# An expert layer on one core: U is split two tiles ahead, ScalarE draws eight one-hot rows per tile, gates are stored in parts

## What is computed

```python
def peer_layer(xn, w_pq, sub_keys, expert_u, expert_v):
    qp = (xt @ w_pq).reshape(t, 8, 2, 128)               # 8 heads, two half queries
    scores = einsum('thpd,hpkd->thpk', qp, sub_keys)      # 128 keys per half
    s_top, i_top = top_k(scores, 16)                      # 16 of each half
    cand = s_top[:, :, 0, :, None] + s_top[:, :, 1, None, :]
    cand_idx = i_top[:, :, 0, :, None] * 128 + i_top[:, :, 1, None, :]
    best, pos = top_k(cand, 16)                           # 16 experts per head
    idx = take_along_axis(cand_idx, pos)
    gate = softmax(best)
    h = gelu(einsum('lkd,ld->lk', expert_u[idx], xb))     # 128 experts per token
    return einsum('lk,lkd->ld', gate * h, expert_v[idx])  # of 16384 experts
```

## Time and profile before

| | before |
|---|---|
| median of 3 runs | 3444.5 us (3442.72 to 3448.07) |
| profiled execution | 3439.6 us, span 3437.8 us |
| TensorE busy | 2902.1 us (84%), 15338 matmuls |
| VectorE busy | 1979.8 us (58%) |
| ScalarE busy | 1083.6 us (32%) |
| GpSimd busy | 824.4 us (24%) |
| mean granted TensorE clock | 0.915 of full speed |
| HBM traffic | 488.49 MB read, 88.21 MB written, 168 GB/s |

### The profile page before, as it was taken

The page is one execution under the profiler, slowest core; times in us unless marked ns, Lnnn a source line. Parts: engine busy times, 40 slices in busy tenths (PEclk is TensorE's granted clock), DMA queues, the critical chain, the costliest instruction groups (busy, mean ns, idle before and its releaser), DMA issues. The chain is left out here.

```text
span 3437.8 us, 40584 instructions
## 1 busy us (share of the span) xinstructions
PE 2902.1 (84%) x15338; PEld 2541.8 (74%) x15338; DVE 1979.8 (58%) x3415; ACT 1083.6 (32%) x1745; POOL 824.4 (24%) x643
## 2 busy tenths in 40 slices
PE   5787669969997878888799999799894869599987
PEld 4787438769996878887688888587673659488877
DVE  4324443337996777645677777545995642444432
ACT  3323442223323323322233333366222432222221
POOL 0002110003325776544423232034330010000000
PEclk8898879989998999999899999899995779799999
DMA  2102012233436776787999999467234532322222
GB/s 105 74 0 76 2 49 98 76 131 126 141 101 197 270 272 237 290 295 274 334 352 357 353 352 354 143 179 230 98 116 139 152 104 85 110 92 93 96 96 82
DMA packets 224065, 578.72 MB, mean 168 GB/s; under 512 B 34896, under 2 KB 126928, under 8 KB 194096
## 3 DMA queue, kind: packets, MB, share of 16 engines
q1 hardware_dynamic: 185184, 434.44, 37.2%
q0 software_dynamic: 36864, 134.23, 10.5%
q10 hardware_dynamic: 1872, 8.13, 0.7%
HBM read 488.49 MB, written 88.21 MB: 168 GB/s over the span
## 5 line engine op out<-in xcount | busy, mean ns | idle before, releaser
L40 PE MATMUL pe_ps<-hh,pe_uh 128*128 128x384 f32 x1024 | 353.5, 345 | 30.9 <-DVE pe_ul L1318 14.4
L41 PE MATMUL pe_ps<-hl,pe_uh 128*128 128x384 f32 x1024 | 347.0, 339 | 0.0
L42 PE MATMUL pe_ps<-hh,pe_ul 128*128 128x384 f32 x1024 | 346.5, 338 | 0.0
L40 PE MATMUL pe_ps<-pe_vh,pe_whi 128*128 128x512 f32 x768 | 300.8, 392 | 22.2 <-DVE pe_vl L1471 22.2
L41 PE MATMUL pe_ps<-pe_vl,pe_whi 128*128 128x512 f32 x768 | 300.4, 391 | 0.0
L42 PE MATMUL pe_ps<-pe_vh,pe_wlo 128*128 128x512 f32 x768 | 300.3, 391 | 0.0
L1279 POOL DMA_INDIRECT pe_gu<-in_u_rows,pe_urow x128 | 186.5, 1457 | 216.1 <-DVE pe_gu L1432 195.2
L1287 POOL DMA_INDIRECT pe_gv<-in_v_w,pe_vrow x128 | 151.7, 1185 | 353.6 <-DVE pe_acc L1441 339.9
L1432 DVE SCALAR_TENSOR_TENSOR pe_gu<-pe_gu,pe_xs 128x1024 f32<-128x1024 f32 x128 | 155.3, 1223 | 122.2 <-DMA pe_gu<-in_u_rows,pe_urow 122.2
L40 PEld LDWEIGHTS pe_ps<-hh,pe_uh 128*128 128x128 f32 x1024 | 196.4, 192 | 34.3 <-ACT pe_uh L1164 19.6
L40 PE MATMUL sc_ps<-hh,sc_wh 128*128 128x512 f32 x512 | 200.0, 391 | 12.6 <-DVE sc_wl L2515 12.6
(11 more groups left out here) (459 smaller groups left out, 7416.3 us busy)
## 6 DMA issues: line engine op xcount, KB each, us to landing
xu<-in_u_w SPq DMA_DIRECT2D x64, 1024.0 KB
pe_v_raw<-in_v_w SPq DMA_DIRECT2D x64, 1024.0 KB, 8.5
sc_raw<-in_sc_w SPq DMA_DIRECT2D x32, 1024.0 KB, 4.9
hidden_scratch<-pe_hs SPq DMA_DIRECT2D x64, 384.0 KB
gate_scratch<-pe_stage SPq DMA_DIRECT2D x6, 4096.0 KB, 19.7
pe_hw<-hidden_scratch SPq DMA_DIRECT2D x64, 384.0 KB
pe_gate<-gate_scratch SPq DMA_DIRECT2D x64, 384.0 KB
gf_raw<-in_gdn_w SPq DMA_DIRECT2D x24, 1024.0 KB, 6.8
```

The lines of the kernel that those rows point to most:

```text
L40: pe.matmul(out, lh, rh, start=start, stop=False)
L41: pe.matmul(out, lh, rl, start=False, stop=False)
L42: return pe.matmul(out, ll, rh, start=False, stop=stop)
```

## The change

- **Split ahead** (`AHEAD` = 2): ScalarE splits tile t+2 before the Gelus of tile t, VectorE makes its low half where it made that of t+3, and SP loads tile t+4 at tile t instead of t+5.
- **Stages**: `A_END` is 22 for 20 and `B_END` 46 for 44, so 22, 24 and 18 tiles. The transposes of the sparse tokens and their copy `xs` move ahead (tile 17 on TensorE, tile 18 on ScalarE).
- **One-hot rows**: ScalarE makes two `second` rows of each group (`DRAWN` = 2, eight a tile) for the next tile: Square(j - iota), then Relu(1 - that). VectorE makes the other eight. GpSimd makes none; it only fetches.
- **Gates in parts**: the 4,096 KB of 64 tokens go in four transfers, over the next three tiles, each ahead of that tile's hidden store.
- **Slots**: from the 85th U row on, five slots instead of three. The rows left after stage B are spread evenly over the 18 tiles.
- **V**: tiles 0 and 1 are loaded at U tiles 57 and 58 and weighed and split at 60 to 63, 2 and 3 are loaded at U tiles 62 and 63, the residual x after all V tiles. The fetched V rows are spread over tiles 2 to 63; before, four came ahead of tile 2.

```diff
@@ constants @@
-    A_END, B_END = 20, 20 + TD // PER
-    POOLED = (1, 2, 1, 2)
+    A_END, B_END = 22, 22 + TD // PER                 # AHEAD, DRAWN = 2, 2
+    EARLY, PARTS = (B_END - A_END) * EACH, 4
+    MORE = EARLY + 4 * EACH
+    def u_slot(s):
+        return s % GU if s < MORE else (s - MORE) % (GU + 2)
@@ SP @@
+                def keep_g(n, part):
+                    if part == 0:
+                        sp.wait_ge(staged, (n + 1) * (GT // Q))
+                    rows = slice(part * NKEYS // PARTS, (part + 1) * NKEYS // PARTS)
+                    sp.dma_start(g_dram[n][:, rows, :], stage[n % 2][:, rows, :]).then_inc(g_out[n % 2], 16)
+                def keep_some(r):
+                    n = r // 4 - 1
+                    for part in ((0, 1), (2,), (3,), ())[r % 4] if n >= 0 else ():
+                        keep_g(n, part)
-                        load_u(t + 5, r + 5, 0)
-                        keep_h(t, r)
-                        if r % 4 == 3:
-                            sp.wait_ge(staged, j * (BODY * Q) + (r + 1) * Q)
-                            sp.dma_start(g_dram[j * 2 + r // 4], stage[r // 4][:]).then_inc(g_out[r // 4], 16)
+                        load_u(t + 2 + AHEAD, t + 2 + AHEAD, 0)
+                        keep_some(t - A_END)
+                        keep_h(t, t)
...
+                    if t in (NU - 7, NU - 6):
+                        load_v(t - NU + 7, t - NU + 7, 0)
                     keep_h(t, t)
+                    if t >= NU - 2:
+                        sp.wait_ge(wv_lo, t - NU + 3)
+                        sp.wait_ge(v_lo, t - NU + 3)
+                        load_v(t - NU + 4, t - NU + 2, 0)
@@ ScalarE @@
+                def draw(it, e):
+                    if it == B_END - A_END:
+                        return
+                    if e:
+                        act.wait_ge(drawn[1], it + 1)
+                    elif it:
+                        act.wait_ge(drawn[3], it)
+                    for b in range(2):
+                        for m in range(DRAWN):
+                            tok = it * PER + (2 * e + b) * Q + m
+                            last = act.activation(gap[:, b, m, :], iota[:], ACT.Square, scale=-1.0, bias=jT[:, tok:tok + 1])
+                    last.then_inc(gap_ok, 1)
+                    act.wait_ge(gap_ok, 2 * it + e + 1)
+                    for b in range(2):
+                        act.activation(second[2 * e + b][:, 0:DRAWN, :], gap[:, b, :, :], ACT.Relu, scale=-1.0,
+                                       bias=iota[:, 1:2]).then_inc(drawn[2 * e + b], 1)
                     for r in range(BODY):
+                        split_u(t + AHEAD, t + AHEAD, 16 * ((t + AHEAD) // 2 + 1))
                         for e in range(UB):
                             gelu(t, t, e, 16 * (t // 2))
-                            if e == UB - 1:
-                                split_u(t + 3, t + 3, 16 * ((t + 3) // 2 + 1))
...
+                            draw(it + 1, e)
@@ GpSimd: the loop with L1297 to L1307 goes @@
+                    if u_last(s):                      # dot of the slot's last row
+                        pool.wait_ge(dot_ok, u_last(s))
+                    elif s >= GU:                      # first use of slots 3 and 4
+                        pool.wait_ge(g_out[1], 16 * PARTS * (TD // GT // 2))
...
+                for s in range(NS):
                     fetch_u(s)
@@ VectorE @@
-                                if m >= POOLED[q]:
+                                if m >= DRAWN:
...
-                        low_u(t + 3, t + 3)
+                        low_u(t + AHEAD, t + AHEAD)
...
-                    for s in range(EACH):
-                        dot((t - A_END) * EACH + s)
+                    if t in (NU - 4, NU - 3):
+                        weigh(t - NU + 4, t - NU + 4, 16)
+                    if t in (NU - 2, NU - 1):
+                        low_v(t - NU + 2, t - NU + 2)
+                    for s in range(upto(NS - EARLY, NU - B_END, t - B_END), upto(NS - EARLY, NU - B_END, t - B_END + 1)):
+                        dot(EARLY + s)
@@ TensorE @@
-                                pe.wait_ge(pooled[q], j * BODY + r + 1)
+                                pe.wait_ge(drawn[q], j * BODY + r + 1)
```

More of the change, by code:

```diff
@@ L993, in peer, with u_turn, u_last, upto @@
     ND, TD = PEER_DENSE, PEER_DENSE * P
-    NS, GU, GV, EACH = PEER_H * PEER_K, 3, 8, 3
+    NS, GU, GV, EACH, AHEAD, DRAWN = PEER_H * PEER_K, 3, 8, 3, 2, 2
     rest = slice(TD, T)
     NU = NKEYS // UB
-    A_END, B_END = 20, 20 + TD // PER
+    A_END, B_END = 22, 22 + TD // PER
     BODY = 8
-    POOLED = (1, 2, 1, 2)
+    EARLY, PARTS = (B_END - A_END) * EACH, 4
+    MORE = EARLY + 4 * EACH
+    def u_slot(s):
+        return s % GU if s < MORE else (s - MORE) % (GU + 2)
+    def u_turn(s):
+        return sum(u_slot(b) == u_slot(s) for b in range(s))
+    def u_last(s):
+        return max((b + 1 for b in range(s) if u_slot(b) == u_slot(s)), default=0)
+    def upto(s, steps, i):
+        return -(-s * i // steps)
     with Phase(nc, "pe") as ph:
@@ L1012, in peer @@
         urow, vrow = (ph.sb(n, [P, NS], U32) for n in ("urow", "vrow"))
-        dots, gs, wts = (ph.sb(n, [P, NS]) for n in ("dots", "gs", "wts"))
+        dots, gs = (ph.sb(n, [P, NS]) for n in ("dots", "gs"))
+        gap = ph.sb("gap", [P, 2, DRAWN, NKEYS])
         area = Arena(nc, ph, 80 * 1024 + 768, "arena")
@@ L1056, in peer @@
         wlo = [area.sb(f"wlo{i}", [P, UB, TD], F32R) for i in range(2)]
+        gu += [area.sb(f"gu{GU + i}", [P, D]) for i in range(2)]
         ps = ph.psum()
@@ L1064, in peer @@
             [ph.sem(f"{n}{i}") for i in range(2)] for n in "u_in h_out keys_in g_out h_in g_in v_in".split())
-        rows_ok, pooled, built = ([ph.sem(f"{n}{i}") for i in range(4)] for n in "rows_ok pooled built".split())
-        (u_hi, u_lo, hid, gelu_ok, zero_ok, cols_ok, staged, x_in, w_ok, wv_hi, wv_lo, v_hi, v_lo, outp, fin, added,
-         stored) = (ph.sem(n) for n in ("u_hi u_lo hid gelu_ok zero_ok cols_ok staged x_in w_ok wv_hi wv_lo v_hi "
+        rows_ok, drawn, built = ([ph.sem(f"{n}{i}") for i in range(4)] for n in "rows_ok drawn built".split())
+        (u_hi, u_lo, hid, gelu_ok, gap_ok, staged, x_in, w_ok, wv_hi, wv_lo, v_hi, v_lo, outp, fin, added,
+         stored) = (ph.sem(n) for n in ("u_hi u_lo hid gelu_ok gap_ok staged x_in w_ok wv_hi wv_lo v_hi "
                                         "v_lo outp fin added stored").split())
@@ L1070, in peer @@
             ph.sem(n) for n in "xsum_ok xs_tr xs_ok row_n rows_known dot_ok act_ok wts_ok acc_ok".split())
-        gu_in, gv_in = ([ph.sem(f"{n}{i}") for i in range(m)] for n, m in (("gu_in", GU), ("gv_in", GV)))
+        gu_in, gv_in = ([ph.sem(f"{n}{i}") for i in range(m)] for n, m in (("gu_in", GU + 2), ("gv_in", GV)))
         pairs = [(n, p) for n in range(NT) for p in range(2)]
@@ L1148, in _ @@
                         load_v(t, r, i)
+                sp.wait_ge(u_lo, NU)
+                sp.dma_start(x[:], load.rearrange("(n p) d -> p n d", p=P)).then_inc(x_in, 16)
                 for m, n in enumerate([ND] + list(range(ND))):
@@ L1172, in _ @@
                 split_q(0)
-                for t in range(3):
+                for t in range(AHEAD):
                     split_u(t, t, 16 * (t // 2 + 1))
@@ L1201, in _ @@
                                 act.dma_start(keys[h % 2][:], keys_dram[h + 2]).then_inc(keys_in[h % 2], 16)
+                    split_u(t + AHEAD, t + AHEAD, 16 * ((t + AHEAD) // 2 + 1))
                     for e in range(UB):
                         gelu(t, t, e, 16 * (t // 2))
-                    split_u(t + 3, t + 3, 16 * ((t + 3) // 2 + 1))
-                    if t == A_END - 2:
+                    if t == 2 * PEER_H + 2:
+                        act.wait_ge(xs_tr, 1)
+                        for half in range(2):
+                            act.activation(xs[:, half * 512:(half + 1) * 512], ps[:, 4 + half, :], ACT.Copy).then_inc(xs_ok, 1)
                         act.wait_ge(sub_ok, 1)
@@ L1422, in _ @@
                 dve.tensor_copy(vrow[:], vrf[:]).then_inc(rows_known, 1)
-                for t in range(2 * PEER_H + 4, A_END + 3):
+                for t in range(2 * PEER_H + 4, A_END + AHEAD):
                     low_u(t, t)
@@ L1428, in dot @@
                 def dot(s):
[L1429 to L1432 removed]
+                    row = gu[u_slot(s)][:]
+                    dve.wait_ge(gu_in[u_slot(s)], 16 * u_turn(s) + 16)
+                    dve.scalar_tensor_tensor(row, row, 1.0, xs[:], ALU.mult, ALU.mult,
                                              accum_out=dots[:, s:s + 1]).then_inc(dot_ok, 1)
```

90 lines of the change are left out of this document (36 added, 54 removed).

## The result

The changed kernel takes 3343.2 us (median of 4 runs, 3338.5 to 3345.0), the kernel before 3443.6 in the same session (3440.0 to 3448.1): a ratio of 0.9706, 95% interval 0.9689 to 0.9722. That is 100.4 us less; 127 were forecast. The profiled execution was the shortest of the four: span 3336.5, and 101.3 us less than the span before.

What follows compares the result with a forecast made beforehand. Waits between engines were taken to hold the expert phase above TensorE's floor. Stage B -74, entry +7, last U tiles -38 and handover -22 gave -127 us: 3318 by the median, forecast range 3295 to 3345, overall range 3283 to 3380.

Steps and rivals of the forecast that it cites:

- Stage B, floor of TensorE: Stage B: hidden and one-hot matmuls hold TensorE 11.9 us a tile.
- ScalarE: Stage B: draws add 4.5 us a tile, making ScalarE 9.5, covered by TensorE's 11.9 if no table is loaded.
- table rivals: Stage B draws load tables: for Relu only, 3375 us, chance 0.05; at every change of function, 3466, slower 0.03.
- VectorE: Stage B: VectorE busy 11.6 us a tile, 12.3 with its remaining wait, so B takes 295 us for 369, -74.
- I let 0.7 stay: Stage B: of VectorE's 1.4 us a tile wait for fetched rows, 0.7 was taken to remain.
- a row is fetched a whole tile (12 us) before use: Stage B: the reason given for letting only 0.7 us a tile of VectorE's wait for fetched rows stay.
- VectorE in order behind its fetched rows: Rival: B's waits stay whole, 13.3 us a tile, last U tiles at 10.5; -76, 3368 us, chance 0.26.
- the two waits of the earlier trace: Stage B: TensorE's 58.5 us for GpSimd's one-hot rows and VectorE's 44.8 us for ScalarE's split, both expected to go.
- Cutting costs nothing in my sum: Gate stores: four 1024 KB transfers take as long as one of 4096 KB, 19.6 us against 19.7; priced at nothing.
- Entry: End of stage A: with two more tiles there, B begins near 1075 us, not 1068; +7 (0 to +14).
- Last tiles: Last U tiles, 18 for 20: DMA is late next, 63 MB at 379 GB/s, 167 us; -38 (-56 to -16).
- Handover: Last U tile to V tile 4: V tiles loaded and split earlier, x later; 38 us for 60, -22 (-12 to -27).

Runs made afterwards that it cites:

- e1: The changed kernel with no fetched rows and no dots in stage B, the first 72 of 128 dots left out; ratio 0.9594.
- c1: The changed kernel with the third dot of a tile in B moved behind VectorE's low half; 3308.2 us, ratio 0.9600.
- e4: The changed kernel with six second rows a tile on GpSimd again and none on ScalarE; 3353.7 us, ratio 0.9726.
- e8: The kernel before with eight second rows a tile drawn on ScalarE, none on GpSimd, weights kept in the gates' tile; 3420.0 us, ratio 0.9919.
- e3: The changed kernel with ScalarE's split of U behind the two Gelus again, still two tiles ahead; 3350.2 us, ratio 0.9706.
- e7: The kernel of e3 with the split made three tiles ahead, as in the kernel before; 3338.6 us, ratio 0.9685.
- e5: The changed kernel with each 64 tokens of gates stored in one transfer of 4096 KB again; 3359.4 us, ratio 0.9745.
- c4: c1 with 23 tiles in stage A, splitting three ahead until its last tile, and two dots in each of the first four tiles behind B; 3296.7 us.
- e6: The changed kernel with three slots for fetched rows to the end, not five behind B; 3370.9 us, ratio 0.9782.
- e9: The changed kernel with the 2 MB of x loaded right behind the last U tile again; 3346.7 us, ratio 0.9710.

## Why the prediction was right, and where not

- **Stage B, floor of TensorE: right.** 11.9 was worked out, and 285.5 / 24 = 11.9 is what e1 and c1 take.
- **ScalarE: right.** 4.4 us of draws for 4.5, and (79.0 + 142.6) / 24 = 9.2 busy a tile for 9.5. Both table rivals are out: Relu and Square run between Gelus without a load. The section on table sets of the Trainium skill cited ahead ("ScalarE: Activation LUTs") agrees for Relu; it doesn't name Square among its fillers.
- **VectorE: nearly right in size, wrong in its wait.** (90.8 + 179.7) / 24 = 11.3 busy for 11.6. "I let 0.7 stay": the wait is 34.3 / 24 = 1.4 a tile, not shorter at all, and over the 1 us that the prediction named as a sign of being wrong. 11.3 and 1.4 are 12.7, the 12.8 measured. The step that failed is "a row is fetched a whole tile (12 us) before use": it counted landing time, not the issue time on GpSimd beside the low half, and not the gate parts beside it. That is the 13 us between 12.3 and 12.8 a tile; e1 and c1 show that the wait holds B. On this wait the rival 'VectorE in order behind its fetched rows' was right.
- **Which part pays: wrong.** The sum laid B's gain to the two waits of the earlier trace rows. The draws give 23 to 27 us (e4, e8). The split's order gives nothing as long as the third fetch holds B at 12.8 a tile, for the old order holds it at 12.9 (e3, e7). Step by step B went from 369.0 to 342.0 (e8, draws) to 317.9 (e7, all but order and depth of the split, with 9 us lost in the first tile) to 307.8, and to 285.5 with c1's dot.
- **Gates in parts: wrong, and partly luck for the total.** "Cutting costs nothing in my sum" was true of bytes, and the gain was priced at nothing too. e5: 23 us in B. Without this unpriced gain B would have missed its forecast by 36 us, not 13. The fixed cost of about 2 us that the Trainium skill gives a transfer ("DMA: Bandwidth & Descriptors", section "Anatomy of one DMA — SWDGE (gpsimd) path") would make 18 more transfers a loss. That section describes GpSimd's path and these stores are SyncE's; here the same bytes in four times as many transfers gain.
- **Entry: right**, +6.6 for +7.
- **Last tiles: mechanism right, size off by 6.** They moved 60 MB (347 GB/s x 173.2 us), 159 us at the 379 GB/s of the sum, so bytes alone don't explain it. All that is over TensorE's 149 is in five stalled tiles that no term held: 49 to 51, which wait for rows fetched with three slots (c4 takes these stalls away), and 61 and 62, beside the loads of V. The slots gain 25 us (e6) and the two tiles fewer 17 at TensorE's pace; together that is 10 more than the 32 measured. Where those went is not shown; V tiles 0 and 1 are now weighed and split in this stage, and 2 and 3 asked for.
- **Handover: right**, 39.7 for 38; x late is worth 5 of it (e9).
- **Behind V: not in the sum.** +8.1 in unchanged code, with 17 us more at the lower clock; the other kernels spread over the same 8 us. No run sets the clock by itself.

From -127: +13 in B, +6 last tiles, +2 handover, +8 behind V, -3 ahead of A: -101.

## What to carry to other kernels

Waits in one stage can't be added: 58.5 us for GpSimd's rows were worth 23 to 27, and 44.8 for the split nothing as long as another stall of the same size stood behind it. So a change that gains nothing when it is taken back may still be needed: look at what the engine waits for then, not at the time alone. For an in-order engine with a ring of slots, count from the end of one use to the start of the next: issue time (and who runs beside it), landing beside everything else on the DMA engines, and compare with the pitch. Before an operation is moved on an engine that runs ahead, look how far ahead it is: its inputs must be ready by that engine's clock.

## What was not expected of the hardware

- An indirect fetch issues on GpSimd in 0.94 us, and in 2.75 when VectorE's 128x2048 subtraction (2.29 us) starts with it. Moving one dot so that the two don't meet took 22 us off stage B.
- One store of 4096 KB delays fetched rows by up to 10.9 us; four of 1024 KB, 11.0 us each to land, by up to 3.0.
- SyncE took 8.3 us in c4 to issue the load of V tile 1, and 2.4 to 2.5 for each of the next two transfers; such issues are mostly 0.3 to 0.5 us elsewhere. The hidden stores behind it landed after 20 to 21 us.
- Identical code behind V took 1246.5 to 1254.6 us, with 289 to 306 us at the lower clock.
